# A transformer layer on one Trainium2 core: the last weight chunk multiplied tile by tile, and the second norm's statistics taken on 128x10 through 32x32 turns

## The reference, cut to what matters

```python
h = layer_norm(ALPHA * x + mix, ln1_g, ln1_b)
u = jnp.square(jax.nn.relu(jnp.einsum('bsd,df->bsf', h, w_ff1) + b_ff1))
f = jnp.einsum('bsf,fd->bsd', u, w_ff2) + b_ff2
return layer_norm(ALPHA * h + f, ln2_g, ln2_b)

def layer_norm(x, g, b):
    mu = x.mean(-1, keepdims=True)
    var = jnp.square(x - mu).mean(-1, keepdims=True)
    return (x - mu) * lax.rsqrt(var + LN_EPS) * g + b
```

## Time and profile before

| what | value |
|---|---|
| median of 3 runs | 1794.14 us (1792.19 to 1795.46) |
| the profiled execution | 1791.96 us |
| its span, first to last instruction | 1790.4 us |
| TensorE busy | 1768.4 us (99%) |
| VectorE busy | 933.8 us (52%) |
| ScalarE busy | 795.3 us (44%) |
| granted TensorE clock, mean | 0.997 |

### The profile page before, as it was taken

One profiled execution on the slowest core, in us unless ns is written; L12 is line 12 of the kernel. 1 busy time (PEld: TensorE's weight loads), 2 busy tenths in 40 slices (PEclk: granted clock), 3 DMA queues, 4 the chain that ended last, 5 costly groups with the idle time before them and its releaser, 6 DMA issues.

```text
span 1790.4 us, 34152 instructions
## 1 busy us (share of the span) xinstructions
PE 1768.4 (99%) x13168; PEld 1742.9 (97%) x13168; DVE 933.8 (52%) x1242; ACT 795.3 (44%) x1136; POOL 142.0 (8%) x268
## 2 busy tenths in 40 slices
PE   9999999999999999999999999999999999999996
PEld 8999999999999999999999999999999999999995
DVE  5555453366666655647776544444444443444465
ACT  5444553456656663335445533443334333334333
POOL 6000010021111111100000000000000000000001
PEclk9999999999999999999999999999999999999998
DMA  9455555587777766655566666666666665666642
GB/s 270 147 156 151 167 168 164 163 314 261 269 251 259 265 224 204 201 174 164 182 209 221 216 223 207 224 202 220 214 213 223 209 222 201 223 202 224 224 150 71
DMA packets 272714, 369.46 MB, mean 206 GB/s; under 512 B 13376, under 2 KB 266496, under 8 KB 269680
## 3 DMA queue, kind: packets, MB, share of 16 engines
q1 hardware_dynamic: 252528, 251.32, 44.9%
q0 software_dynamic: 10752, 107.38, 15.6%
q10 hardware_dynamic: 9344, 9.51, 1.6%
HBM read 356.02 MB, written 70.71 MB: 238 GB/s over the span
## 4 chain that ended last, share of the span: by engine, by line
PE 96%; DMA 2%; DVE 1%; ACT 0%; POOL 0%; issue 0%; SPq 0%; ACTq 0%
PE psM L1394 30%; PE psM L1393 30%; PE psM L1395 30%; DMA s_raw<-in_w_in_dram 1%; PE psM L1483 1%; PE psT L1495 1%; PE psO L1539 1%; DMA s_kca<-in_kT_a_dram 1%; PE psT L1413 0%; PE psO L1520 0%; PE psO L1529 0%; PE psM L1465 0%; PE psM L1472 0%; DVE s_r L1377 0%; PE psT L1500 0%; PE psT L1393 0%
## 5 line engine op out<-in xcount | busy, mean ns | idle before, releaser
L925 DVE TENSOR_TENSOR s_wlo<-s_raw,s_whi 128x1024 fp32r<-128x1024 f32 x467 | 571.5, 1227 | 657.9 <-ACT s_whi L525 652.5
L525 ACT ACTIVATE s_whi<-s_raw 128x1024 fp32r<-128x1024 f32 x467 | 492.7, 1058 | 810.7 <-PE psM L1395 787.8
L1393 PE MATMUL psM<-s_xhi,s_whi 128*128 128x320 f32 x1184 | 371.2, 313 | 0.0
L1395 PE MATMUL psM<-s_xhi,s_wlo 128*128 128x320 f32 x1184 | 365.8, 309 | 0.0
L1394 PE MATMUL psM<-s_xlo,s_whi 128*128 128x320 f32 x1184 | 365.7, 309 | 0.0
L1393 PE MATMUL psM<-s_uhi,s_whi 128*128 128x320 f32 x1024 | 316.9, 309 | 0.0
L1394 PE MATMUL psM<-s_glo,s_whi 128*128 128x320 f32 (+1 forms) x1024 | 316.7, 309 | 0.0
L1395 PE MATMUL psM<-s_uhi,s_wlo 128*128 128x320 f32 x1024 | 316.4, 309 | 0.0
L1394 PE MATMUL psM<-s_ulo,s_whi 128*128 128x320 f32 x1024 | 316.4, 309 | 0.0
L1395 PE MATMUL psM<-s_ghi,s_wlo 128*128 128x320 f32 (+1 forms) x1024 | 316.0, 309 | 0.0
L1393 PE MATMUL psM<-s_ghi,s_whi 128*128 128x320 f32 (+1 forms) x1024 | 315.9, 308 | 0.0
(11 more groups left out here) (259 smaller groups left out, 1768.0 us busy)
## 6 DMA issues: line engine op xcount, KB each, us to landing
s_raw<-in_w_ff_dram SPq DMA_DIRECT2D x256, 512.0 KB, 3.8
s_raw<-in_w_in_dram SPq DMA_DIRECT2D x155, 512.0 KB, 3.9
s_kvbuf<-in_kT_b_dram POOLq DMA_DIRECT2D x8, 2448.0 KB, 9.4
s_kvbuf<-in_v_b_dram POOLq DMA_DIRECT2D x8, 2304.0 KB, 8.3
s_raw<-in_w_out_dram SPq DMA_DIRECT2D x32, 512.0 KB, 3.4
out_b_s_dram<-in_cache_b_kv_dram POOLq DMA_DIRECT2D x16, 1008.0 KB, 7.0
s_raw<-in_w_branch_a_dram SPq DMA_DIRECT2D x16, 512.0 KB, 3.6
gates_scratch<-s_gstage ACTq DMA_DIRECT2D x16, 320.0 KB, 4.3
```

The lines of the kernel that those rows point to most:

```text
L525: act.activation(whi[:, slot], raw[:, slot], ACT.Copy).then_inc(hi_done, 1)
L925: dve.tensor_tensor(wlo[:, slot], raw[:, slot], whi[:, slot].bitcast(F32), ALU.subtract).then_inc(lo_done, 1)
L1393: pe.matmul(out, wh, xh, start=first and k == 0, stop=False)
L1395: mm = pe.matmul(out, wl, xh, start=False, stop=last and k == KT - 1)
```

## The change

The last chunk is no longer multiplied by `chunk` but by a new function `tile_by_tile`, with the tiles outside and the blocks inside: the 12 matmuls of tile 14 first, with a semaphore of their own (`tile_done`), then the 12 of tile 15. DVE adds tile 14 while TensorE multiplies tile 15, and adds `r[:, 14]` to `lnrow[:, 0]` and its square to `lnrow[:, 1]` (semaphore `sums_14`). The row sum of `lnrow[:, 0]` stands ahead of the last three matmuls of tile 15, that of `lnrow[:, 1]` behind them, and only tile 15 has row sums of its own.

The 320 means and mean squares stand alike in all partitions. DVE's `transpose` turns each 32x32 square of a 128x320 operand; after it, column 32b of the result holds token 32b + p%32 in partition p. Taking one column of each square gives 128x10 operands, `cols`, on which the square of the mean, the variance, the root (ACT) and the reciprocal are made. A third turn, of the reciprocal repeated 32 times along the free axis, lays it out over 320 columns in `psT`. The subtraction for tiles 2 and 3 moves behind the first multiplication, and ACT's square of `delta` goes.

```diff
@@ ScalarE
             act.activation(delta, psO[:, 0, 0:NTOK], ACT.Copy).then_inc(delta_in, 1)
-            act.wait_ge(delta_in, 2)
-            act.activation(dsq, delta, ACT.Square).then_inc(dsq_in, 1)
             act.wait_ge(var_in, 2)
-            act.activation(std, lnrow[:, 2], ACT.Sqrt, bias=eps[:, 0:1]).then_inc(root_in, 1)
+            act.activation(cols[:, 2], cols[:, 1], ACT.Sqrt, bias=eps[:, 0:1]).then_inc(root_in, 1)
@@ VectorE
+            dve.wait_ge(tile_done, 1)
+            dve.tensor_tensor(r[:, 14], r[:, 14], psM[0][:, 0, 0:NTOK], ALU.add).then_inc(tail_d, 1)
+            dve.wait_ge(part_sums, 4)
+            dve.wait_ge(tail_d, 1)
+            dve.tensor_tensor(lnrow[:, 0], lnrow[:, 0], r[:, 14], ALU.add).then_inc(sums_14, 1)
+            dve.wait_ge(tail_sq, 1)
+            dve.tensor_tensor(lnrow[:, 1], lnrow[:, 1], t2[:, 1, 0], ALU.add).then_inc(sums_14, 1)
             dve.wait_ge(chunk_done, B3 + 32)
-            for t in (14, 15):
-                dve.tensor_tensor(r[:, t], r[:, t], psM[0][:, t - 14, 0:NTOK], ALU.add).then_inc(tail_d, 1)
+            dve.tensor_tensor(r[:, 15], r[:, 15], psM[0][:, 1, 0:NTOK], ALU.add).then_inc(tail_d, 1)
             shift = psO[:, 0:1, 0:NTOK].broadcast_to([P, 2, NTOK])
             dve.wait_ge(delta_in, 2)
+            dve.transpose(t1[:, 0], delta).then_inc(across, 1)
+            dve.wait_ge(across, 1)
+            mean, meansq = (t1[:, k].rearrange("p (b c) -> p b c", b=10)[:, :, 0] for k in range(2))
+            dve.tensor_tensor(cols[:, 0], mean, mean, ALU.mult).then_inc(dsq_in, 1)
+            dve.wait_ge(stat_sq, 2)
+            dve.transpose(t1[:, 1], psO[:, 1, 0:NTOK]).then_inc(across, 1)
+            dve.wait_ge(dsq_in, 2)
+            dve.wait_ge(across, 2)
+            dve.tensor_tensor(cols[:, 1], meansq, cols[:, 0], ALU.subtract).then_inc(var_in, 1)
             dve.tensor_tensor(r[:, 0:2], r[:, 0:2], shift, ALU.subtract).then_inc(less_d, 1)
-            dve.wait_ge(stat_sq, 2)
-            dve.wait_ge(dsq_in, 2)
-            dve.tensor_tensor(lnrow[:, 2], psO[:, 1, 0:NTOK], dsq, ALU.subtract).then_inc(var_in, 1)
-            dve.tensor_tensor(r[:, 2:4], r[:, 2:4], shift, ALU.subtract).then_inc(less_d, 1)
             dve.wait_ge(root_in, 2)
-            dve.reciprocal(psT[:, 0, 0:NTOK], std).then_inc(rstd_in, 1)
+            dve.reciprocal(cols[:, 3], cols[:, 2]).then_inc(across, 1)
+            dve.wait_ge(across, 3)
+            dve.transpose(psT[:, 0, 0:NTOK], cols[:, 3].rearrange("p (b c) -> p b c", c=1).broadcast_to([P, 10, 32])).then_inc(rstd_in, 1)
             dve.wait_ge(rstd_in, 2)
             for k, (lo, hi) in enumerate(MULS):
+                if k == 1:
+                    dve.tensor_tensor(r[:, 2:4], r[:, 2:4], shift, ALU.subtract).then_inc(less_d, 1)
@@ TensorE
+            def tile_by_tile(c):
+                pe.wait_ge(lo_done, c + 1)
+                for t in range(2):
+                    for k in range(KT):
+                        if t == 1 and k == KT - 1:
+                            pe.wait_ge(sums_14, 1)
+                            row_sum(mean_d, lnrow[:, 0], True, False)
+                        wh, wl = (w[:, 3, k, P * t:P * t + P] for w in (whi, wlo))
+                        out, xh, xl = psM[0][:, t, 0:NTOK], uhi[:, 12 + k], ulo[:, 12 + k]
+                        pe.matmul(out, wh, xh, start=False, stop=False)
+                        pe.matmul(out, wh, xl, start=False, stop=False)
+                        mm = pe.matmul(out, wl, xh, start=False, stop=k == KT - 1)
+                    mm.then_inc(*((tile_done, chunk_done)[t], 1))
...
-                    chunk(B3 + 4 * g + j, j, psM[par], uhi, ulo, 4 * j, j == 0, j == 3)
+                    if g == 7 and j == 3:
+                        tile_by_tile(B3 + 4 * g + j)
+                    else:
+                        chunk(B3 + 4 * g + j, j, psM[par], uhi, ulo, 4 * j, j == 0, j == 3)
-                    if g == 7 and j == 2:
-                        pe.wait_ge(part_sums, 4)
-                        row_sum(mean_d, lnrow[:, 0], True, False)
-                        row_sum(mean_sq, lnrow[:, 1], True, False)
-            for t in (14, 15):
-                pe.wait_ge(tail_d, t - 13)
-                mm = row_sum(mean_d, r[:, t], False, t == 15)
-            mm.then_inc(stat_d, 1)
-            for t in (14, 15):
-                pe.wait_ge(tail_sq, t - 13)
-                mm = row_sum(mean_sq, t2[:, 1, t - 14], False, t == 15)
-            mm.then_inc(stat_sq, 1)
+            pe.wait_ge(sums_14, 2)
+            row_sum(mean_sq, lnrow[:, 1], True, False)
+            pe.wait_ge(tail_d, 2)
+            row_sum(mean_d, r[:, 15], False, True).then_inc(stat_d, 1)
+            pe.wait_ge(tail_sq, 2)
+            row_sum(mean_sq, t2[:, 1, 1], False, True).then_inc(stat_sq, 1)
```

More of the change, by code:

```diff
@@ L119, in program @@
         eps = sb("eps", [P, 2])
+        cols = sb("cols", [P, 4, 10])
         st = sb("st", [P, 3, 16])
@@ L171, in program @@
         delta_in, dsq_in, var_in, root_in, rstd_in = (sem(n) for n in ("delta_in", "dsq_in", "var_in", "root_in", "rstd_in"))
+        tile_done, sums_14, across = sem("tile_done"), sem("sums_14"), sem("across")
         less_d, less_p, mul_d, y_act, y_dve = (sem(n) for n in ("less_d", "less_p", "mul_d", "y_act", "y_dve"))
```

## The result

The changed kernel takes 1795.86 us (median of 17 runs, 1793.58 to 1798.9), the kernel before 1793.13 (17 runs, 1790.95 to 1795.73): ratio 1.0016 with a 95% interval of 1.001 to 1.0023, slower by 0.16%. The prediction said 1792.5 and a range that ends at 1794.8, so the time lies above it. (Counted from the 1793.13 of these runs, the forecast gain of 1.6 would have been 1791.5.) The profiled execution took 1794.8 us.

A forecast was written before the change was run, and what follows sets the result against it. The end was taken as fixed by when tile 7 is ready, starting the full store stream. Gains 1.09 + (4.05 - 2.73) = 2.41 us, less 0.8, gave 1.6: 1794.14 - 1.6 = 1792.5 us, range 1790.0 to 1794.8.

The forecast's parts named there:

- with ten elements I take 0.17: DVE between mean and first multiplication: a 128x10 operation lies between 0.16 and 0.49 us, taken as 0.17.
- POOL does not stand in the way: Scaling of the tiles after the statistics: POOL's first piece (2.88 us) ends near 1775.5, so it delays nothing.
- Forecast 1.09 us at ACT's copy: From the last chunk to the mean: ACT's copy of the mean starts at 1772.00 instead of 1773.09.
- The wait that I had costed at nothing: PE's wait for tile 14's sums inside the last chunk: no cost, cover 0.1 us; rival of a stall, chance 0.07.
- Turns: Three DVE transposes of 128x320 between mean and first multiplication: 0.49 us each, bounds 0.33 to 2.15.
- turns dearer than 1.02: Rival, DVE between mean and first multiplication: turns cost more than they save, 1797.5 us at 2.15 each; chance 0.06.
- a square before it writes: Rival, inside each turn: filling and emptying do not overlap, 0.83 us a turn, gain 0.6, 1793.5 us; chance 0.13.
- the sum at S: S is the start of DVE's first multiplication after the reciprocal (1777.61 before); claimed 2.41 us earlier, at 1775.20.
- What is put back: Subtraction for tiles 2 and 3, moved behind the first multiplication, takes 0.8 us off the gain, leaving 1.6.
- the store model: End of the kernel: full write stream begins 0.97 us after the second store's issue and lasts 5.5 us.
- the stores hide it: Rival, final stores: DMA engines full from the first store on, so earlier tiles gain nothing, 1794.1 us; chance 0.04.
- no change that can be measured: Whole-kernel outcome within 0.2% (3.6 us) of before; chance 0.85, against 0.12 faster and 0.03 slower.

The follow-up runs named there:

- pool_later: Changed kernel with POOL's subtractions waiting for the variance instead of the mean; tail 22.96 us, -0.91 against before, ratio 0.9992 (0.9983 to 1.0).
- one_sbuf_input: Changed kernel with ACT squaring the mean and the second turn writing PSUM; tail 22.25 us, -1.62 against before, ratio 0.9991 (0.9982 to 1.0).
- before_two_sbuf: Kernel before with DVE's two subtractions reading the mean from its SBUF copy instead of PSUM; tail 26.18 us, +2.31 against before, one execution.

## Why the prediction was wrong

**The step that failed** is the term "with ten elements I take 0.17" for the two 128x10 operations, together with "POOL does not stand in the way". The trace has 2.50 and 2.30 us instead of 0.17 each, 4.46 us more, and without it the tail falls below that of before, as pool_later (-0.91) and one_sbuf_input (-1.62) show. I had bounded the size of the operation (0.16 to 0.49) and looked at POOL only for what waits for its results, not for what it holds while it runs. In the tail of the kernel before, each two-input DVE operation beside POOL has one operand in PSUM (the mean and the mean square in `psO`, the reciprocal root in `psT`), so no row of the tail could show the wait; the change put both operands of two operations into SBUF. No rival named this: all four spoke of turns, PE and stores.

The trace of the kernel before did show the wait, though far from the tail. DVE's L925 makes `wlo` from two inputs in SBUF, 467 times; here are its shortest, median and longest time in ns, and POOL's copy and the longest L925 in the timeline:
```profile
L925 DVE TENSOR_TENSOR s_wlo<-s_raw,s_whi x467: 1162/1226/1753, 10.8 to 1757.2; 128x1024 fp32r<-128x1024 f32 x156
```
```profile
258.50 1.11 POOL L395 COPY s_kTb<-s_tT 128x512 f32 x1 [12.55 <-DVE s_tT L1011]
258.76 1.75 DVE L925 TENSOR_TENSOR s_wlo<-s_raw,s_whi 128x1024 fp32r<-128x1024 f32 x1 [0.45 <-ACT s_whi L525]
```
All five executions of L925 above 1.28 us ran beside a copy of POOL. A rival could have been priced from such rows before the result was known.

The Trainium skill says this outright (SBUF — State Buffer, "SBUF: two separate sides" and "Who interferes with whom"): a DVE instruction with two SBUF inputs shares a port pair with a GpSimd instruction that reads SBUF, and whichever starts first keeps it for its whole instruction. The traces agree wherever the runs tried it: 2.50 and 2.30 us beside pieces of 2.88, 1.16 and 0.96 beside pieces of 1.53 and 1.52, 0.17 with one input from PSUM, and POOL held in its turn in before_two_sbuf. It was the rule that spoke against this change, and I did not weigh it.

**The other steps**, by the same rows:
- *TensorE.* Forecast 1.09 us at ACT's copy; it came 0.95 earlier (5.61 us after the start of the tail, 6.56 before). The wait that I had costed at nothing cost 0.13: the row sum in the last chunk took 0.67 instead of 0.54. Two things used up the cover of 0.1. DVE's second add started at 1768.63, 0.10 behind the end of the first (1768.04 + 0.49), not 0.03. And the forecast counted PE's matmuls from the chain's 1766.53, where the timeline of the kernel before has the row sums start at 1766.37, so PE asked 0.16 earlier than the forecast said.
- *Turns.* 0.49 us forecast; 0.51, 0.51 and 0.53 measured, from and into SBUF or PSUM. The rivals "turns dearer than 1.02" and "a square before it writes" (0.83) fall. By the Trainium skill (VectorE: DVE Perf Modes, The three transpose paths) a turn has SBUF as its target and my estimate scaled from its 311 ns was 0.78; rows here have PSUM as the target too and show 0.49 to 0.53, and the measurement decides.
- *Reciprocal on 128x10* 0.20 (forecast 0.22); with one input in PSUM, or with POOL idle, the 128x10 operations take 0.17 to 0.18, as forecast. pool_later, which has every DVE operation of the change and no lock, tests the sum at S: 2.13 us earlier than before (8.95 against 11.08), where 2.41 was forecast. Of the missing 0.28, half is the later copy of the mean, and half lies between DVE's start and S (2.87 instead of 2.73).
- *What is put back, and the stores.* In one_sbuf_input S comes 8.72 us after the start of the tail (1776.17 from 1767.45), before 11.08: a gain of 2.36 where 2.41 was forecast, and 1.62 of it at the end, where 1.6 was. That closeness is in part luck: this kernel has one DVE operation fewer than the forecast one (ACT makes the square), which makes up for most of the 0.28. The 0.8 put back behind S is borne out in the changed kernel itself: from S to the second store 6.22 us, before 5.42. In the changed kernel the store model holds too: second store issued at 1785.87, full stream from 0.93 us later, 5.5 us long.
```profile
1785.87 0.39 SPq L362 DMA_DIRECT2D out_yT_dram<-s_r  x1
```
```profile
1786.60:1786.80 0.20, 0.00 (x0) 0.00 (x0) 0.20 (x1) 0.20 (x2) 0.00 (x0) 0.50 0.02 6
1786.80:1787.00 0.20, 0.00 (x0) 0.00 (x0) 0.20 (x1) 0.20 (x2) 0.00 (x0) 0.50 0.85 307
...
1792.20:1792.40 0.20, 0.00 (x0) 0.00 (x0) 0.00 (x0) 0.00 (x0) 0.00 (x0) 0.50 0.68 231
```
The rows answer to the earlier trace rows. So "the stores hide it" falls as well: nothing swallowed the gain, a new wait of 4.46 us turned it over.
- *The chances.* The prediction gave 0.85 to "no change that can be measured", and the time did stay within its 0.2%, at 0.16% slower. That is luck: it expected a gain of 1.6 us, and what came is that gain and a larger loss that it did not have.

## What to carry to other kernels

For every new DVE operation with two inputs, ask where both lie and what GpSimd runs at that moment: with both in SBUF the price, on top of the operation's own time and whatever its size, is about what is left of GpSimd's instruction, and one operand in PSUM avoids it. A duration read from a row holds only beside the same neighbours; where a change puts an operation beside an engine that no row shows it beside, that is a rival to be priced, and rows elsewhere in the same trace may have the price, as L925's did here. Once the tail is shortened, look for the next limits (the last store's issue, a hole between stores) before counting on more.

## What the runs showed of the hardware that was not expected

- A ten-column operation waits as long as a large one. With 2.47 us of GpSimd's instruction left, the 128x10 square took 2.33 longer than its own 0.17; with 2.43 left, the 128x640 subtraction of before_two_sbuf took 2.29 longer than its 0.81. The row counts the wait as busy time, with no idle time ahead of it. In the profile such a hold looks like a slow instruction, not like a wait.
- DVE's turn of 128x320 in 32x32 squares takes 0.49 to 0.53 us whether SBUF or PSUM is its source or its target.
- DVE's add with two waits ahead of it started 0.10 us behind its predecessor, where small operations follow after 0.03. The turn and the difference of the changed kernel show the same 0.10 (1775.80 to 1775.90), again with two waits between, but L1394, also with two, follows its turn after 0.03 (1779.62 to 1779.65). So the second wait alone is not the cause. In the two slow places the wait that is met last stands second, in the quick one first; no run changed that order.
